# When a token tile's queries and keys are turned in the first attention of a two-layer encoder step

## The reference

```
q, k, v, g = jnp.split(h @ w_in, 4, axis=-1)
q = _rope(q.reshape(b, t, A_HEADS, 2, A_DH), pos)
k = _rope(k.reshape(b, t, A_HEADS, 2, A_DH), pos)
...
s = jnp.einsum('bqhcd,bkhcd->bhcqk', qb.astype(f32), kf) * (A_DH ** -0.5)
mask = k_chunk[None, :] <= (qpb // CHUNK)[:, None]
pr = jax.nn.softmax(jnp.where(mask, s, NEG_INF), axis=-1)
w = pr[:, :, 0] - lam * pr[:, :, 1]
return jnp.einsum('bhqk,bkhe->bqhe', w, vf)
```

## Time and profile before

| | |
|---|---|
| median of 3 runs | 1870.46 us (1869.45 to 1871.29) |
| profiled execution's own time | 1870.63 us |
| its span, first to last instruction | 1868.8 us |
| mean granted TensorE clock | 0.986 of full |
| busy PE / PEld | 1754.2 us (94%) / 1561.5 us (84%) |
| busy DVE / ACT / POOL | 987.7 (53%) / 853.8 (46%) / 555.6 (30%) us |

### The profile page before, as it was taken

The page is one execution under the profiler, slowest core; times in us unless marked ns, Lnnn a source line. Parts: engine busy times, 40 slices in busy tenths (PEclk is TensorE's granted clock), DMA queues, the critical chain, the costliest instruction groups (busy, mean ns, idle before and its releaser), DMA issues. The chain is left out here.

```text
span 1868.8 us, 30233 instructions
## 1 busy us (share of the span) xinstructions
PE 1754.2 (94%) x11315; PEld 1561.5 (84%) x11315; DVE 987.7 (53%) x1740; ACT 853.8 (46%) x2054; POOL 555.6 (30%) x709
## 2 busy tenths in 40 slices
PE   4999999999999989999979999999999999799996
PEld 3878788787888868999978888888888888599995
DVE  5455564645556463234437475655747565643335
ACT  5354554645456453223335454544545454622225
POOL 0131322313132210015714343434434343500442
PEclk9999999999999999999989999999999999899998
DMA  4112211111221123222122022020212112252213
GB/s 158 44 52 64 69 37 56 41 52 52 64 69 41 52 99 109 84 65 90 61 68 64 30 64 62 31 75 25 80 35 64 58 35 63 88 153 83 58 44 135
DMA packets 161505, 124.85 MB, mean 67 GB/s; under 512 B 10960, under 2 KB 152336, under 8 KB 161360
## 3 DMA queue, kind: packets, MB, share of 16 engines
q1 hardware_dynamic: 160496, 122.72, 21.3%
q10 hardware_dynamic: 864, 0.20, 0.0%
HBM read 89.36 MB, written 33.52 MB: 66 GB/s over the span
## 5 line engine op out<-in xcount | busy, mean ns | idle before, releaser
L107 PE MATMUL pj<-h_high,area 128*128 128x384 f32 (+1 forms) x1536 | 378.7, 332 | 10.8 <-issue 5.2
L1511 POOL TENSOR_TENSOR lb_a<-lb_a,lb_remain 128x127 f32<-128x127 f32 (+3 forms) x192 | 237.3, 1255 | 365.9 <-DVE lb_remain L1385 258.5
L107 PE MATMUL pj<-area,h_high 128*128 128x384 f32 (+1 forms) x1152 | 332.9, 351 | 7.2 <-issue 5.5
L107 PEld LDWEIGHTS pj<-h_high,area 128*128 128x128 f32 x1536 | 264.5, 190 | 13.4 <-issue 10.7
L107 PE MATMUL pj<-h_low,area 128*128 128x384 f32 (+1 forms) x768 | 249.2, 324 | 0.0
L1385 DVE TENSOR_TENSOR_SCAN lb_remain<-lb_remain 128x512 f32<-128x512 f32 (+4 forms) x200 | 198.7, 1031 | 67.6 <-ACT lb_remain L1228 66.8
L1228 ACT ACTIVATE lb_remain<-lb_sc 128x512 f32<-128x512 f32 (+4 forms) x200 | 100.0, 500 | 264.1 <-PE lb_sc L1592 233.7
L107 PEld LDWEIGHTS pj<-area,h_high 128*128 128x128 f32 (+1 forms) x1152 | 203.8, 181 | 19.7 <-issue 5.6
L107 PE MATMUL pj<-area,h_low 128*128 128x384 f32 (+1 forms) x576 | 195.1, 339 | 0.0
L107 PEld LDWEIGHTS pj<-h_low,area 128*128 128x128 f32 x768 | 145.4, 189 | 0.0
L757 POOL TENSOR_TENSOR la_ra<-la_tok,cos 128x64 f32<-128x64 f32 (+1 forms) x72 | 23.1, 321 | 337.2 <-ACT la_tok L438 337.2
(11 more groups left out here) (294 smaller groups left out, 3815.2 us busy)
## 6 DMA issues: line engine op xcount, KB each, us to landing
stage<-in_a_w_in SPq DMA_DIRECT2D x60, 192.0 KB, 3.3
stage<-in_b_w_in SPq DMA_DIRECT2D x60, 192.0 KB, 3.1
stage<-in_ple_w_gate SPq DMA_DIRECT2D x22, 512.0 KB, 3.7
h_low<-o_t SPq DMA_DIRECT2D x14, 528.0 KB, 6.4
mix_b_xs<-x_mid SPq DMA_DIRECT2D x8, 528.0 KB
lift_xt<-in_x SPq DMA_DIRECT2D x8, 512.0 KB, 4.2
stage<-in_a_w_in SPq DMA_DIRECT2D x16, 256.0 KB, 5.1
out_ak<-la_tok SPq DMA_DIRECT2D x8, 512.0 KB, 3.3
```

Of the source, the lines that this page charges most:

```text
L107: last = pe.matmul(out, x, y, start=start and n == 0, stop=stop and n == 2, **kw)
L1511: pool.tensor_tensor(out, out, after, ALU.mult).then_inc(S["a"], 1)
```

## The change

The turning of tile j - 1 is taken out of the run of products of tile j and put behind it, in steps 2 to 8. In step 9 it stays between the two halves of the gate's products. The past keys are turned in the bank `acc`, where the value sums are made, and no longer in `pj[:, 1]`; with that the wait for the past keys' low part goes from `free_bank(7)` to `values(0)`, and the past transposes wait for the former group's norm (the last reader of `acc`) and no longer for the turned tile 5.

```diff
-        past_bank = pj[:, 1, :]
+        past_bank = acc[:, :]
...
                     if c == 0:
-                        pe.wait_ge(S["normed"], at.before("normed"))
+                        pe.wait_ge(S["past_low"], at.all("past_low"))
...
                     else:
                         pe.wait_ge(S["turned_low"], at.nth("turned_low", t - 1))
-                    if t == PAST_AT + 1:
-                        pe.wait_ge(S["past_low"], at.all("past_low"))
...
-                    if j <= 9:
-                        turn(at, j - 1)
+                    if j == 9:
+                        turn(at, 8)
...
                     if j <= 8:
                         project(at, j, LATE)
+                        turn(at, j - 1)
...
                     if j == PAST_AT:
                         pe.wait_ge(S["past"], at.nth("past", 32))
-                        pe.wait_ge(S["turned_low"], at.nth("turned_low", PAST_AT))
+                        pe.wait_ge(S["normed"], at.before("normed"))
```

## The result

The changed kernel took 1877.55 us (median of 6 runs, 1876.64 to 1879.42) against 1870.26 us of the kernel before in the same runs: ratio 1.0038, 95% interval 1.0025 to 1.0051. It is slower by 7.3 us, and the forecast had been 9.8 us slower. The profiled execution has a span of 1875.7 us, 6.9 more than before, at the same mean clock of 0.986.

What follows compares the result with a forecast made beforehand. PE, busy 94% of the span, was taken to bound the kernel through its line of starts. Seams -0.6, new wait +11.7 and past keys -1.3 gave +9.8 us on 1870.46: 1880.3 us, range 1876 to 1885.

Steps and rivals of the forecast that it cites:

- the 20.4 us for combined weights: PE's waits in the whole span: largest said to be for DVE's combined weights, 20.4 us in 15 times.
- The wait that comes in: Next tile's product waits for the turned tile's low part: 0.62, 0.55, 0.29 us in steps 2 to 4; +11.7 us.
- the chain's last link: Hand-over from DVE's end to PE's product: 0.15 us, of 1.41 us from first transpose to product.
- Step 5 without a wait: Step 5, transpose to next tile's product: 1.41 us of chain against 1.41 without a wait, so wait 0.
- The seams: PE from the tile's 15th product to scores: 2.07 us before, 2.06 after; 0.01 saved a step, 56 steps, -0.6 us.
- some 2.7 us lower: Transposes to scores: with weights loaded early, the seam would be 0.03 us, not 0.20, and the sum about 2.7 lower.
- The past keys: Tile 7's first product no longer waits for the past keys' low part: 0.16 us, times 8, -1.3 us.
- The sum: Whole kernel: -0.6 + 11.7 - 1.3 = +9.8 us, forecast 1880.3 us.
- The later waits don't absorb it: Rival: PE's steps 10 and 11 waits for combined weights absorb the new wait; 1868.6 us, no change; chance 0.04.
- The new waits don't bring the clock down: Rival: new waits drop PE's clock, one half-clock stretch a group costing 11 us; 1891 us; chance 0.04.
- DVE doesn't come out ahead: Rival: DVE's chain of steps 9 to 11 ends sooner, removing 20.4 us of PE waits; 1860 us; chance 0.03.

## Why the prediction was right

The side, the place and the mechanism were right; the forecast time was 2.7 us too high (1880.3 for 1877.55), inside the range. One reading was wrong without bearing on the sum: the largest wait of PE in the whole span is not the 20.4 us for combined weights but one of 22.3 us in the second layer (L1618 for POOL's L1511).

- **The wait that comes in, +11.7 us.** The mechanism is shown by the run with the other bank. The term was mis-sized in the chain's last link, "from DVE's end to PE's product the same kind of wait shows 0.15". It was not the same kind. Tile 7's first product in the kernel before had two waits ahead of it, for the turned tile and for the past keys, and the second, which blocked, was an instruction of its own; a product with one wait starts 0.06 us behind DVE's end. The two runs with two waits show that this is the difference. With 1.31 for 1.41 the waits of steps 2 to 4 are 0.52, 0.45 and 0.20, 1.17 us a group, 9.4 us in all, 2.3 less than forecast. The run with the other bank gives 1.21 a group, 9.6 us. The rest of the chain, 1.26 us, was right to the hundredth.
- **Step 5 without a wait** was right: 1.39 us, its own cover.
- **The seams, -0.6 us.** Right: the scores start 0.31 behind the first transpose. The runs with the turning behind the products in four steps and in all seven, without a wait, are both 0.05 us a group below the one with none, 0.4 us in all. Transposes to scores are 0.20 apart and not 0.03: in step 3 of the changed kernel the scores' weight load starts with the scores, as it did before:

```profile
150.93 0.19 PEld L851 LDWEIGHTS la_sc<-la_qk_high 64*128 64x128 f32 x2 [0.17 <-issue]
```

  The Trainium skill (TensorE: Matmul & The Clock Gate, "Step-by-step: what each phase is for") lets a weight load that goes to the background buffer be pulled ahead of running products. The row shows no such load here, and no run shows the time some 2.7 us lower that the prediction worked out for that case.
- **The past keys, -1.3 us.** Measured 0.18 a group, 1.5 us, by itself.
- **The sum.** With the waits at their measured size, 9.4 - 0.6 - 1.3 = 7.5 us; by the period it is 7.8, and the medians differ by 7.3. That the terms and the medians agree so closely is in part luck. Up to the first past transposes the changed kernel's profile is 1.4 us behind, in the seven periods up to the eighth group it loses 6.8 more, and behind those it gains 0.9, so that the last products of the layer start 7.3 us later:

```profile
709.02 0.30 PE L903 MATMUL la_sc<-la_sq,la_mean 128*128 128x32 f32 x2
```
```profile
716.34 0.30 PE L903 MATMUL la_sc<-la_sq,la_mean 128*128 128x32 f32 x2
```

  Of the 0.9, the past keys explain 0.2. The other 0.7 are not a gain of the change that any run shows: in the last group, where PE has waits of up to 3.3 us before and 3.2 changed, the granted clock falls to its lower level (1.2 GHz) for about 10 us in both kernels, and it falls on different work. Before, and then in the changed kernel:

```profile
693.80:703.90 10.10, 8.34 (x20) 4.41 (x21) 6.78 (x11) 5.28 (x11) 1.86 (x2) 0.50 0.78 320
```
```profile
694.00:697.20 3.20, 3.20 (x13) 3.20 (x14) 1.59 (x3) 2.28 (x4) 0.94 (x1) 0.50 0.02 5
697.40:704.00 6.60, 3.76 (x25) 3.24 (x25) 6.36 (x15) 4.18 (x10) 0.75 (x1) 1.00 0.38 128
704.20:710.80 6.60, 5.78 (x14) 2.73 (x13) 4.55 (x6) 4.16 (x8) 0.93 (x1) 0.50 1.02 413
```

  From its past transposes to its last products the last group takes 56.08 us before, 55.20 in the changed kernel, 56.05 in the run with the past keys' part alone and 55.04 in the run with the other bank. That the place of the lower clock makes this difference was not tested by itself. PE's wait for moved weights (L473) doesn't explain it: it shrinks from 1.5 to 0.9 us in the changed kernel, but it is 0.9 in the run that takes 56.05 us and 1.5 in the one that takes 55.04.
- **The rivals.** The later waits don't absorb it: L665's row is 19.9 us for 20.4. The new waits don't bring the clock down: it is 1.00 from 82 to 661 us, with three of them a group, and 1.00 from 87 to 695 us with the six a group, up to 1.0 us long, of the run with the turning behind the scores. The lower level in the last group is there in the kernel before too. DVE doesn't come out ahead.

## What to carry to other kernels

A transpose put behind a run of products isn't free of the run: count from it to the next writer of its bank, and compare with what PE does in between; here 1.31 us of chain met 0.79, 0.86 and 1.11 of cover, and 1.40 in the next step, where nothing was lost. Before giving up such an order, look for a bank that lies idle in that stretch: the same order with another bank was 1.21 us a group faster. And when a hand-over is taken from a row, check how many waits stand ahead of the instruction in it, and which of them blocks.

## What the runs showed of the hardware

- A product that waits for one semaphore starts 0.06 us behind the end of the DVE instruction that it waits for (151.94 for 151.88 in the changed kernel). With a second wait ahead of it, the blocking one an instruction of its own, it starts 0.09 us later (1.40 for 1.31 from transpose to product); with the blocking wait on the weight load it is 1.31 again.
- Breaking a run of products by two transposes costs about as much as putting them between the run and 64-row score products: 0.01 us a step between the two orders (periods of 81.07 and 81.02 us).
- Two transposes directly behind 64-row scores start 0.17 us apart (the run with the turning behind the scores), behind 128-row products 0.11 (the changed kernel).
- The first weight load of 64-row scores starts with the scores themselves, 0.25 us after the last load behind 128-row products and 0.17 behind transposes (step 4 before, step 3 changed); it is not done early in either place.
